# State-space branch: input scalings, decay exponents and state products in another order, with four buffers instead of two

## The reference, cut to what matters

```
h_t = exp(dt_t A) h_{t-1} + dt_t x_t B_t^T,   y_t = h_t C_t

cum  = cumsum(log_a)                      # per chunk
lmat = masked exp(cum[t] - cum[s])
y    = (C B^T * lmat) (x dt) + (C exp(cum)) s
s    = exp(cum[-1]) * s + (x dt exp(cum[-1] - cum))^T B
```

## Time and profile before

| what | value |
|---|---|
| three executions | 1523.97, 1528.56, 1524.31 us |
| median | 1524.31 us |
| profiled execution, span from first to last instruction | 1525.0 us |
| its own time beside the span | none is listed; the span stands for it |
| mean granted TensorE clock, share of full speed | 0.986 |
| instructions | 19389 |

### The profile page before, as it was taken

How to read it: one execution, slowest core, us unless ns; L and a number is a source line. 1 busy time by engine, 2 the same in 40 slices (tenths; PEclk the granted TensorE clock), 3 DMA queues, 4 the chain that set the end, 5 groups by cost and what they waited for, 6 DMA issues and landing times. The chain is left out here.

```text
span 1525.0 us, 19389 instructions
## 1 busy us (share of the span) xinstructions
PE 1467.5 (96%) x7408; PEld 929.8 (61%) x7408; DVE 460.4 (30%) x980; ACT 394.8 (26%) x898; POOL 86.4 (6%) x76
## 2 busy tenths in 40 slices
PE   6999999999989999999999988999999999999996
PEld 2565677676866666677866855554455555555553
DVE  3337232752144236322110352321111121121114
ACT  3212112221343243222311231222222322222223
POOL 0000010000011103221111000000000000000001
PEclk9999999999999999999999989999999999999998
DMA  8540423213112328510134225699999999899981
GB/s 325 189 116 12 140 65 110 83 56 119 47 56 83 124 83 338 173 56 28 61 110 133 87 107 230 248 421 390 376 377 376 373 363 373 350 376 376 377 347 42
DMA packets 104608, 308.64 MB, mean 202 GB/s; under 512 B 9711, under 2 KB 69864, under 8 KB 76136
## 3 DMA queue, kind: packets, MB, share of 16 engines
q1 hardware_dynamic: 97424, 303.59, 52.2%
q10 hardware_dynamic: 7128, 4.27, 1.0%
HBM read 304.70 MB, written 3.15 MB: 202 GB/s over the span
## 5 line engine op out<-in xcount | busy, mean ns | idle before, releaser
L543 PE MATMUL banks<-hT,ring 128*128 128x384 f32 x1216 | 400.3, 488 | 2.3 <-ACT hT L1117 2.3
L543 PEld LDWEIGHTS banks<-hT,ring 128*128 128x128 f32 x1216 | 230.7, 191 | 157.5 <-issue 2.7
L2418 PE MATMUL banks<-w,xg 128*64 128x512 f32 (+1 forms) x1312 | 233.1, 594 | 1.5 <-issue 0.3
L2418 PEld LDWEIGHTS banks<-w,xg 128*64 128x64 f32 (+1 forms) x1312 | 79.1, 126 | 151.6 <-issue 142.5
L2456 PE MATMUL banks<-w,hidT 128*64 128x512 f32 (+1 forms) x656 | 120.7, 598 | 0.3 <-ACT hidT L2497 0.2
L2330 PE MATMUL banks<-y,selT 128*128 128x512 f32 x384 | 104.4, 407 | 0.0
L2330 PEld LDWEIGHTS banks<-y,selT 128*128 128x128 f32 x384 | 67.4, 189 | 37.5 <-issue 26.2
L543 PE MATMUL banks<-yT,ring 128*128 128x384 f32 x256 | 88.3, 491 | 0.7 <-issue 0.7
L543 PE MATMUL banks<-ring,hT 128*128 128x256 f32 x384 | 86.2, 387 | 0.0
L2597 DVE TENSOR_TENSOR y<-banks,y 128x512 fp32r<-128x512 f32 x66 | 45.6, 691 | 133.0 <-ACT y L2513 133.0
L543 PEld LDWEIGHTS banks<-ring,hT 128*128 128x128 f32 x384 | 74.6, 195 | 10.4
(11 more groups left out here) (400 smaller groups left out, 1433.7 us busy)
## 6 DMA issues: line engine op xcount, KB each, us to landing
w<-in_exp_w SPq DMA_DIRECT2D x198, 1024.0 KB, 8.7
ring<-in_w_in SPq DMA_DIRECT2D x46, 1024.0 KB, 5.3
ring<-in_ada_w SPq DMA_DIRECT2D x24, 1024.0 KB, 6.7
ring<-in_w_branch SPq DMA_DIRECT2D x8, 1024.0 KB, 6.7
ring<-in_w_out SPq DMA_DIRECT2D x4, 1024.0 KB, 6.4
arena<-in_sh_w SPq DMA_DIRECT2D x3, 1024.0 KB, 7.7
x<-in_x_sample SPq DMA_DIRECT2D x2, 512.0 KB, 11.9
out_y_sample<-x SPq DMA_DIRECT2D x2, 512.0 KB, 2.6
```

Of the source, the lines that this page charges most:

```text
L543: last = mm(out, lhsT=lhsT, rhs=rhs, start=i == 0, stop=i == len(pairs) - 1)
L2418: ins = mm(ps[lo:hi, :], lhsT=xg[:, k, a_ * P + lo:a_ * P + hi], rhs=w13[:, a_, u, :, k, :], start=k == 0, stop=k == KD - 1)
```

## The change

`sxd` gets four buffers, one per direction and w. TensorE computes the four groups of decay exponents of tile 0 behind the transposes of `sin`, ahead of the state products; its waits for `s_masks` and for the freeing of `rows` move there with them. `prepare(t)` computes exponents only for t > 0, and its wait for the last state bank stands ahead of `sinter` in place of ahead of everything; the wait for `sin` goes. VectorE scales all four inputs first and takes the states of both directions after that; its waits for the state products of direction 0 go.

```diff
-        sxd = part(6 * U + 512, 2, W)
+        sxd = part(6 * U + 512, 2, 2, W)
...
+            def both_decays(t):
+                for d in range(2):
+                    for q in range(2):
+                        decay(mm, banks, pe, ("sdec", t, d, q), ident_r[:, :], reach[:, d, :],
+                              pick_row[:, d * 8 + q * 4:d * 8 + q * 4 + 4], decay_rows[:, tok[t]])
+
+            pe.wait_ge(s_masks.sem, 3)
+            banks.emptied(pe, "rows")
+            both_decays(0)
+            banks.emptied(pe, ("sb", NT - 1))
             for d in range(2):
                 for w, t in ((0, 0), (1, FIRST[d])):
-                    banks.emptied(pe, ("sb", NT - 1))
                     pe.wait_ge(s_sxe.sem, 2 * d + w + 1)
...
-                            last = mm(ps[:, i * P:(i + 1) * P], lhsT=sxd[:, w, i * P:(i + 1) * P],
+                            last = mm(ps[:, i * P:(i + 1) * P], lhsT=sxd[:, d, w, i * P:(i + 1) * P],
...
-            banks.emptied(pe, ("sstate", 1, 1))
-            banks.emptied(pe, ("sin", 1))
             def prepare(t):
...
-                for d in range(2):
-                    for q in range(2):
-                        decay(mm, banks, pe, ("sdec", t, d, q), ident_r[:, :], reach[:, d, :],
-                              pick_row[:, d * 8 + q * 4:d * 8 + q * 4 + 4], decay_rows[:, tok[t]])
                 if t:
+                    both_decays(t)
+                    banks.emptied(pe, ("sstate", 1, 1))
...
-            pe.wait_ge(s_masks.sem, 3)
-            banks.emptied(pe, "rows")
             prepare(0)
...
             for d in range(2):
                 for w, t in ((0, 0), (1, FIRST[d])):
-                    if d:
-                        banks.at(dve, ("sstate", 0, w))
-                    s_sxe.on(tt(heads8(sxd[:, w, :]), heads8(sxN[:, t, :]), each(dte[:, t, d * 8:d * 8 + 8]), ALU.mult))
-                if d == 0:
-                    take_states(dve, nc, banks, lane, 0, snew, sst, ecum, small_cols, FIRST, halves4, heads8)
-            take_states(dve, nc, banks, lane, 1, snew, sst, ecum, small_cols, FIRST, halves4, heads8)
+                    s_sxe.on(tt(heads8(sxd[:, d, w, :]), heads8(sxN[:, t, :]), each(dte[:, t, d * 8:d * 8 + 8]), ALU.mult))
+            for d in range(2):
+                take_states(dve, nc, banks, lane, d, snew, sst, ecum, small_cols, FIRST, halves4, heads8)
```

More of the change, by code:

```diff
@@ L832, in _ @@
                             last = mm(ps[:, i * 256:(i + 1) * 256], lhsT=sbN[:, t, i, :],
-                                      rhs=sxd[:, w, i * 256:(i + 1) * 256], start=True, stop=True)
+                                      rhs=sxd[:, d, w, i * 256:(i + 1) * 256], start=True, stop=True)
                     banks.close(last)
-            banks.emptied(pe, ("sstate", 1, 1))
-            banks.emptied(pe, ("sin", 1))
             def prepare(t):
```

## The result

| | before | changed |
|---|---|---|
| median, six runs each | 1527.43 us | 1519.12 us |
| least and most | 1523.97 to 1530.73 | 1510.25 to 1520.06 |
| profiled span | 1525.0 | 1518.3 |
| mean granted clock in the profiled run | 0.986 | 0.987 |

The ratio of changed to before is 0.9938, 95% interval 0.9914 to 0.9962: faster by 0.4% to 0.9%. The first medians differ by 8.3 us, the profiled spans by 6.7 us. The forecast was 1518.3 us with 5.95 us of gain.

The account below looks back on a forecast made before the run. TensorE, busy 1467.5 of 1525.0 us, was taken as the bound. Idle 4.55 plus clock 1.41 gave 5.96 (5.95 by the new list), so 1524.31 - 5.95, rounded to 1518.3 us; range 1516.6 to 1522.4.

Parts of the forecast that it names:

- The time, 1518.3 us: Whole kernel: 1524.31 less 5.95 us, rounded; given 55%.
- 0.69 below that span: Starting time: median of the runs shown taken as 0.69 us below the profiled span of 1525.0, giving 1524.31.
- Exponents first: TensorE behind the `sin` transposes: 0.37 us idle left of 1.12, then four exponent groups in 2.75 us without bank waits.
- State products, 4.00 us: TensorE behind the exponents: twelve matmuls per direction, 2.00 us each at full clock, from 427.97 to 431.97.
- Clock, 1.41 us: Direction 1's state products: full clock once the 2.22 us wait goes, 3.41 to 2.00 us; bounds 0 and 1.41.
- idle only: Rival: only the idle is gained, 4.55 us, for 1519.8 us; 17%.
- L840's wait, 1.58 us: TensorE ahead of C B^T: the 1.58 us wait for the last state bank goes; the moved wait costs nothing.
- Is `sintra` ready?: Both weighings end near 435.1, TensorE comes at 437.6: 2.5 us to spare; contention 0.3 on VectorE, 0.45 on GpSimd.
- Behind the stage nothing gives the gain back: Behind `sintra` (L865): TensorE busy for 116.41 us at full clock, so the gain is not waited for again.
- Doesn't do what it says: Rival: states were hidden anyway, `sintra` waits for weighed decays, time stays 1524.3 us; 5%.
- slower by a clock that stays low: Rival: low clock from exponents through lift, 12.42 us of full-clock work, up to about 1530.8 us; 5% with others.
- Part given back: Rival: 2 to 4 us lost further on, between 850 and 900 us, for 1520.3 to 1522.3 us; 13%.

Follow-up runs that it names:

- the second set: Changed kernel run again unchanged beside the kernel before: median 1518.18 us beside 1524.96, ratio 0.9957, `sin` transposes to `sintra` 13.35 us.
- `busy_gap`: Kernel before plus two fp32 matmuls, result overwritten, in TensorE's wait between the directions: `sin` transposes to `sintra` 18.41 us, ratio 0.9965.
- `tensor_part_only`: Changed kernel with two input buffers and VectorE's old order, TensorE's new order kept: `sin` transposes to `sintra` 18.45 us, ratio 0.9961.
- `longer_vector_chain`: Changed kernel plus six VectorE copies between the taking of states and first weighing: `sin` transposes to `sintra` 14.27 us; one run.
- `filled_wait`: Changed kernel plus four unread fp32 matmuls in TensorE's wait ahead of the shared expert: median 1516.19 us, ratio 0.9930.
- `totals_early`: Changed kernel with VectorE's total-decay multiplications moved straight behind the four scalings: `sin` transposes to `sintra` 13.34 us, ratio 0.9957.
- `bank_wait_back`: Changed kernel with waits for last state bank and `sin` bank back ahead of tile 0's C B^T: `sin` transposes to `sintra` 15.98 us, ratio 0.9975.
- `exponents_behind`: Changed kernel with the first exponents back behind state products and C B^T: `sin` transposes to `sintra` 14.08 us, ratio 0.9955.

## Why the prediction was right, point by point

- **The time, 1518.3 us.** That it is 0.8 us from the median of 1519.12 is in part luck. The median of the kernel before, from which the gain was taken off, was 1524.31 us over three runs and 1527.43 over six; the medians are 8.3 us apart, those of the second set 6.8, and the forecast gain was 5.95. The distance in the traces is what bears the terms out. The step "0.69 below that span" compares two measures: in the runs with both, the time is 1.8 us above the span (1520.06 for 1518.3). The gain doesn't use it.
- **Exponents first: idle 0.37 us left, 2.75 us of work.** Measured 0.40 and 428.17 - 425.43 = 2.74. No bank was waited for. Alone the move is worth 0.73 us.
- **State products, 4.00 us.** Measured 431.73 - 428.17 = 3.56. This is the one term of the sum that was off by more than 0.1 us. I took each direction as the time from its first start to its last end, 2.00 us, but matmuls that follow on overlap with the end of those before: from first start to first start it is 1.81 and 1.75 us. Of the 0.48 us between the forecast gain of 5.95 and the 6.43, this is 0.44.
- **Clock, 1.41 us.** Borne out in the traces, as to size and, with the reserve named at `busy_gap`, as to cause: both traces of the changed kernel have the full clock through the stage, and `busy_gap` gave 1.37 us back by work of no use. In the trace of the kernel before the clock is at 0.50 from 430.7 on, only 0.5 us behind the start of direction 1's products, and in full again from 434.0. In how many executions of the kernel before the clock falls here can't be had from its one trace, and `tensor_part_only` shows it falling elsewhere. So the rival "idle only", 4.55 us, is not settled for the executions without a trace. The medians, 8.3 and 6.8 us apart, and the ratio of `busy_gap` speak against it. At equal mean clock the two kernels are 4.9 us apart, near the idle and overlap terms together (4.52 + 0.44), but that comparison leaves the clock's share out from the start and doesn't decide it.
- **L840's wait, 1.58 us.** Gone. Had it been left where it was it would have cost 2.36 us of idle.
- **Is `sintra` ready?** The weighings were forecast for about 435.1 and ended at 435.40, with TensorE forecast at 437.64 and there at 437.34. The room was 1.9 us by the trace and 1.8 by `longer_vector_chain`, not 2.5. 0.3 of the difference is TensorE's overlap, and 0.3 VectorE's end. Its 435.1 held nothing for the contention. I had set 0.3 us aside for that, and L2782 took 1.31 us for 0.69, 0.62 more; the products also started 0.20 later (428.17 for 427.97), and VectorE's operations that follow on directly took about 0.5 us less than laid out. GpSimd's share, 0.45 us, was right.
- **Behind the stage nothing gives the gain back.** From `sintra` to the end it is 1080.96 us for 1081.41. The same stretch is 1080.6 in the second trace, and between 1077.4 and 1079.9 in the traces of the experiments, `filled_wait` left aside (1078.7 there): these differences are not the change's, and the clock between 850 and 935 us differs with them (0.90 in the changed kernel, 0.96 in `longer_vector_chain`, which has 1077.4). That they come from where a run's clock falls is borne out by the line of time on clock and by the shared expert's 64 matmuls, 21.38 us in three traces of kernels that edit nothing there and 22.26 to 23.77 in seven; each of them was not traced back.
- **The rivals.** "Doesn't do what it says" and "slower by a clock that stays low" are refuted by the two traces of the changed kernel. "Part given back" didn't show; its price, a few us by the clock behind the stage, is the size of what differs from run to run, so that a single pair of runs could have looked like it.

## What to carry to other kernels

A wait of the engine that bounds the kernel costs more than its length: here 4.5 us of idle came with 1.4 us at half clock and 0.4 us of lost overlap, and the whole is read by laying out the engine's new list from first start to first start. Buffers and order should be changed together and priced together, since either alone left a longer wait in the place of the other's (3.15 us for 2.22, and 1.97 for 1.58). Where runs differ by more than the change is worth, compare a distance between two fixed instructions in the traces and put the times against the granted clock. And before a change of the clock is put down to an edit, look at the same place in the traces of kernels without that edit.

## What the runs showed of the hardware

- A two-input SBUF operation of VectorE beside a GpSimd add: 1.31 us for 0.69, and the two adds 2.95 for 2.50, in all six traces with this overlap (1.30 to 1.32, and 2.94 or 2.95); apart from each other in `totals_early`, neither. The Trainium skill, "SBUF — State Buffer", section "SBUF: two separate sides", says that the later of the two waits for the whole of the earlier one when VectorE has two inputs in SBUF and GpSimd reads from SBUF. The trace of the changed kernel agrees as to who waits, but not for how long. A single add takes 1.27 us, so the first would end at 429.74 + 1.27 = 431.01 and L2782, 0.69 us alone, at 431.70; it ended at 430.25 + 1.31 = 431.56. The second add, from 430.97 on, would then wait for all of L2782's 0.69 us; it took 1.72 us for 1.27, 0.45 more.
- The clock fell behind waits of 2.22 us (before) and 3.15 us (`tensor_part_only`), and did not behind one of 2.36 us in `bank_wait_back`, whose lift took 5.16 us (433.76 to 438.92) as at full clock. Ahead of the shared expert it fell behind waits of 3.25 us (`bank_wait_back`, 22.26 us for the 64 matmuls) and 3.93 us (`exponents_behind`, 22.57), and did not behind 3.90 us (`longer_vector_chain`, `totals_early`, 21.38). So the length of a single wait does not decide it.
